# Multiplying the expert weights into identity blocks on GpSimd, ahead of ScalarE's diagonals

## The reference, cut to what matters

```python
def one_chunk(args):                       # 128 tokens
    hc, ec, gc = args                      # tokens, expert indices (128, 8, 16), softmax weights
    pre = jnp.einsum('cd,chkd->chk', hc, u[ec]).astype(jnp.float32)
    coef = (gc * jax.nn.gelu(pre, approximate=False)).astype(h.dtype)
    return jnp.einsum('chk,chkd->cd', coef, v[ec])
```

## Time and profile before

| what | value |
|---|---|
| three runs | 2333.66 us median (2331.21 to 2335.54) |
| profiled execution | 2334.32 us, span of its instructions 2332.6 us |
| PE, PEld, DVE busy | 84%, 58%, 60% of the span |
| ACT, POOL busy | 46%, 25% |
| gathers | from 354.4 us on; the last matmul of a row ends at about 1957 us |
| mean granted TensorE clock | 0.905 |

### The profile page before, as it was taken

How to read it: one execution, slowest core, us unless ns; L and a number is a source line. 1 busy time by engine, 2 the same in 40 slices (tenths; PEclk the granted TensorE clock), 3 DMA queues, 4 the chain that set the end, 5 groups by cost and what they waited for, 6 DMA issues and landing times.

```text
span 2332.6 us, 41079 instructions
## 1 busy us (share of the span) xinstructions
PE 1959.3 (84%) x16124; PEld 1344.2 (58%) x16124; DVE 1395.7 (60%) x3264; ACT 1074.3 (46%) x2533; POOL 582.4 (25%) x541
## 2 busy tenths in 40 slices
PE   5888897988888779877855988889888885999999
PEld 4767785655545546545522623356665553667887
DVE  6654678686776676656577576666555533123554
ACT  3334545455555652224344758634454213343443
POOL 0000003332223343334344234433333330000000
PEclk8999998998888889998966996689999997999999
DMA  9932449998889999999999999999999994313555
GB/s 343 340 123 73 162 136 386 390 385 340 322 326 409 402 418 418 417 419 418 417 418 414 410 396 402 382 418 417 418 417 418 418 418 173 137 46 127 183 180 169
DMA packets 140497, 758.52 MB, mean 325 GB/s; under 512 B 16224, under 2 KB 22496, under 8 KB 74384
## 3 DMA queue, kind: packets, MB, share of 16 engines
q0 software_dynamic: 74784, 543.30, 57.1%
q1 hardware_dynamic: 60864, 208.23, 24.0%
q10 hardware_dynamic: 4656, 4.36, 0.6%
HBM read 751.60 MB, written 4.23 MB: 324 GB/s over the span
## 4 chain that ended last, share of the span: by engine, by line
PE 44%; DMA 30%; ACT 10%; DVE 10%; issue 4%; POOL 2%; ACTq 0%; SPq 0%; DVEq 0%
DMA arena<-experts,eidx 27%; PE psum L1324 7%; PE psum L842 4%; DVE arena L2475 4%; PE psum L843 4%; PE psum L844 4%; PE psum L1172 4%; DMA ring<-w_stream 2%; POOL arena L2452 2%; PE psum L1448 2%; PE psum L1621 2%; PE psum L1498 2%; DVE ring_low L2495 2%; ACT arena L2096 1%; PE psum L1197 1%
## 5 line engine op out<-in xcount | busy, mean ns | idle before, releaser
L2475 DVE CUSTOM_DVE_ANT_0 arena<-arena 128x1024 f32<-128x1024 f32 (+3 forms) x592 | 691.6, 1182 | 398.5 <-DMA arena<-experts,eidx 372.1
L2452 POOL DMA_INDIRECT arena<-experts,eidx x512 | 573.6, 1120 | 1203.8 <-PE psum L1324 925.6
L1324 PE MATMUL psum<-arena,sq 32*32 32x512 f32 x8192 | 372.2, 710 | 278.4 <-ACT sq L2104 265.6
L2090 ACT ACTIVATE arena<-arena 128x2 f32<-128x2 f32 x256 | 51.8, 202 | 585.5 <-DVE arena L2475 582.7
L1324 PEld LDWEIGHTS psum<-arena,sq 32*32 32x32 f32 x8192 | 84.4, 110 | 402.7 <-ACT sq L2104 351.0
L1172 PE MATMUL psum<-arena,ring 128*128 128x256 f32 x976 | 235.5, 396 | 4.1 <-ACT arena L1945 4.1
L1172 PEld LDWEIGHTS psum<-arena,ring 128*128 128x128 f32 x976 | 187.3, 197 | 77.1 <-issue 47.3
L1643 PE MATMUL psum<-arena,ring 128*128 128x256 f32 x704 | 162.6, 386 | 0.7 <-DVE arena L2472 0.7
L842 PE MATMUL psum<-hn_high,w_high 128*128 128x256 f32 (+1 forms) x416 | 127.8, 307 | 39.6 <-DVE ring_low L2495 21.7
L1643 PEld LDWEIGHTS psum<-arena,ring 128*128 128x128 f32 x704 | 131.2, 191 | 48.6 <-issue 31.0
L2104 ACT ACTIVATE sq<-sq,arena 128x32 f32<-128x32 f32 x512 | 136.6, 314 | 23.8
(11 more groups left out here) (377 smaller groups left out, 3380.6 us busy)
## 6 DMA issues: line engine op xcount, KB each, us to landing
ring<-w_stream SPq DMA_DIRECT2D x340, 512.0 KB
arena<-w_ada SPq DMA_DIRECT2D x48, 512.0 KB, 7.2
arena<-experts,eidx POOLq DMA_INDIRECT x512
arena<-cum_rows POOLq DMA_DIRECT2D x1, 2112.0 KB, 10.2
x<-xT SPq DMA_DIRECT2D x2, 1024.0 KB, 8.5
arena<-rel_rows ACTq DMA_DIRECT2D x4, 512.0 KB, 12.7
arena<-rel_rows POOLq DMA_DIRECT2D x1, 1024.0 KB, 10.7
k_early<-arena POOLq DMA_DIRECT2D x2, 512.0 KB, 6.3
```

The source lines that it names most:

```text
L1324: last = mm(bank(4 + 2 * odd + a)[QUART * b:QUART * b + QUART, :], diag[k, s, :], rows[k, s, D + a * 512:D + (a + 1) * 512], start=c == 0, ...
L2090: steps(op(pre[:, s:s + 2], pre[:, s:s + 2], ACT.Gelu))
L2452: nc.gpsimd.indirect_dma_start(rows[:, s, :], None, experts, bass.IndirectOffsetOnAxis(ap=eidx[:, n // P % 2, n % P:n % P + 1], axis=0)).t ...
L2475: return V.tensor_tensor_reduce(out=out, in0=a, in1=b, scale=1.0, scalar=0.0 if op1 == ALU.add else -TAKEN, op0=op0, op1=op1, accum_out=accum)
```

## The change

GpSimd gets an instruction for each pair of rows: it multiplies `ident_quart` by the two columns of `wgt`, into a new buffer `weighted_ident` of 8 blocks of 32 columns (the last 256 columns of `sq`). ScalarE makes the diagonals from these blocks, scaled by the Gelu in `pre`; its two multiplications into `coef` go. The waits for `weighed` and `pair_ready` move from ACT to POOL. POOL's order is: gathers 0 to 7, the blocks for rows 0 to 7, then gather(n), and after each even one weigh(n). A block is free again when ACT has made the diagonals of the two rows that used it 8 rows before.

```diff
+        weighted_ident = sq_flat[:, SQ_FREE + T:SQ_FREE + T + SLOT * QUART].rearrange("p (a b) -> p a b", b=QUART)
...
                 steps(op(pre[:, s:s + 2], pre[:, s:s + 2], ACT.Gelu))
-                if n % PK == 0:
-                    act.wait_ge(weighed.sem, weighed.ready(n // PK))
-                steps.wait()
-                for c in range(2):
-                    k = (n + c) % P
-                    steps(op(coef[:, s + c:s + c + 1], pre[:, s + c:s + c + 1], ACT.Copy,
-                             scale=wgt[:, n // P % 2, k:k + 1]))
                 if n >= SLOT:
                     act.wait_ge(rows_used.sem, rows_used.free(n + 1, SLOT))
+                act.wait_ge(ident_weighed.sem, ident_weighed.ready(n // 2))
                 steps.wait()
-                if n == 0:
-                    act.wait_ge(pair_ready.sem, pair_ready.ready(0))
                 for c in range(2):
-                    op(diag[:, s + c, :], ident_quart, ACT.Copy, scale=coef[:, s + c:s + c + 1]).then_inc(diag_done.sem, 1)
+                    op(diag[:, s + c, :], weighted_ident[:, s + c, :], ACT.Copy, scale=pre[:, s + c:s + c + 1])\
+                        .then_inc(diag_done.sem, 1)
...
+            def weigh(n):
+                s, k = n % SLOT, n % P
+                if n == 0:
+                    pool.wait_ge(pair_ready.sem, pair_ready.ready(0))
+                if n % PK == 0:
+                    pool.wait_ge(weighed.sem, weighed.ready(n // PK))
+                if n >= SLOT:
+                    pool.wait_ge(diag_done.sem, diag_done.free(n + 1, SLOT))
+                nc.gpsimd.tensor_tensor(weighted_ident[:, s:s + 2, :], ident_quart.unsqueeze(1).to_broadcast([P, 2, QUART]),
+                                        wgt[:, n // P % 2, k:k + 2].unsqueeze(2).to_broadcast([P, 2, QUART]), ALU.mult)\
+                    .then_inc(ident_weighed.sem, 1)
...
-            for n in range(HEADS * PK):
+            for n in range(SLOT):
                 gather(n)
+            for n in range(0, SLOT, 2):
+                weigh(n)
+            for n in range(SLOT, HEADS * PK):
+                gather(n)
+                if n % 2 == 0:
+                    weigh(n)
```

More of the change, by code:

```diff
@@ L675, in program @@
         diag_done = signal("act", "diag_done")
+        ident_weighed = signal("pool", "ident_weighed")
         rows_used = signal("pe", "rows_used")
@@ L2090, in diagonals @@
                 steps(op(pre[:, s:s + 2], pre[:, s:s + 2], ACT.Gelu))
-                if n % PK == 0:
-                    act.wait_ge(weighed.sem, weighed.ready(n // PK))
+                if n >= SLOT:
+                    act.wait_ge(rows_used.sem, rows_used.free(n + 1, SLOT))
+                act.wait_ge(ident_weighed.sem, ident_weighed.ready(n // 2))
                 steps.wait()
                 for c in range(2):
-                    k = (n + c) % P
-                    steps(op(coef[:, s + c:s + c + 1], pre[:, s + c:s + c + 1], ACT.Copy,
-                             scale=wgt[:, n // P % 2, k:k + 1]))
-                if n >= SLOT:
-                    act.wait_ge(rows_used.sem, rows_used.free(n + 1, SLOT))
-                steps.wait()
-                if n == 0:
-                    act.wait_ge(pair_ready.sem, pair_ready.ready(0))
-                for c in range(2):
-                    op(diag[:, s + c, :], ident_quart, ACT.Copy, scale=coef[:, s + c:s + c + 1]).then_inc(diag_done.sem, 1)
+                    op(diag[:, s + c, :], weighted_ident[:, s + c, :], ACT.Copy, scale=pre[:, s + c:s + c + 1])\
+                        .then_inc(diag_done.sem, 1)
             def sum_out(j):
@@ L2454, in gather @@
                     bass.IndirectOffsetOnAxis(ap=eidx[:, n // P % 2, n % P:n % P + 1], axis=0)).then_inc(rows_ready[s], 16)
-            for n in range(HEADS * PK):
-                gather(n)
+            def weigh(n):
[4 more added lines that the diff above has]
+                    pool.wait_ge(weighed.sem, weighed.ready(n // PK))
+                if n >= SLOT:
+                    pool.wait_ge(diag_done.sem, diag_done.free(n + 1, SLOT))
[3 more added lines that the diff above has]
+            for n in range(SLOT):
+                gather(n)
+            for n in range(0, SLOT, 2):
[4 more added lines that the diff above has]
+                    weigh(n)
             pool.wait_ge(cum_ready.sem, cum_ready.ready(1))
```

## The result

The changed kernel is faster: 2315.75 us median of 7 runs (2307.74 to 2324.1) against 2331.59 us of the kernel before in 7 runs (2331.21 to 2338.36), ratio 0.993, 95% interval 0.991 to 0.9951. A second set, 10 runs beside 33 of the kernel before, gave 2315.86 against 2333.66 us, ratio 0.992 (0.9891 to 0.9949). Ratios leave out single runs over 1.5% above the fastest of their kernel, medians are of all runs. The profiled execution took 2315.75 us, its span 2314.0.

What follows compares the result with a forecast made beforehand. Full DMA queues were taken to bound the kernel, gains coming only where transfers rest. The terms 6.6 - 1.6 + 2.0 + 0.55 + 0.5 - 0.9 = 7.15 us off 2334.32 gave 2327 us, ratio 0.997, range 2317 to 2337.

Steps and rivals of the forecast that it cites:

- What bounds the kernel: Row loop: full DMA queues set the time; only stretches where DMA rests can gain, 40.6 us of rest in all.
- The part that goes: Between Gelu and diagonal on ScalarE: without the copies, 0.55 us less for each pair on the chain.
- 520 to 700 us: Early resting stretch: 12 chain passes at 0.55 us, 6.6 us, less 1.6 us taken back by other work.
- 1380 to 1500 us: Late stretch: 8 chain passes, 4.4 us, DMA resting only 4.3 us; 2.0 us taken, bounds 0 and 4.3.
- rival 3: 520 to 700 and 1420 to 1500 us: fewer stalls keep TensorE's clock up; 17 us in all, 2317 us; chance 0.12.
- The halves that were assumed: Resting stretches: only 20 chain passes counted at 0.55 us, 6.6 us cut by a quarter, 4.4 us to 2.0.
- The part that is added: GpSimd's 256 multiplications: 0.6 us each with gap, delay hidden by queue or row ahead; held dots cost 0.9 us.
- The port: Shared SBUF ports: a two-input VectorE instruction and a GpSimd one wait for each other; at most 12 us over 40 pairs.
- rivals 4 and 5: VectorE held by the multiplication in resting stretches, 2344 us, chance 0.09; POOL becoming the bound everywhere, 2462 us, chance 0.05.
- The tail and the rest: Last pair, copy between last Gelu and last matmuls: 0.55 us; remaining small DMA rests: 0.5 us, bounds 0 and 7.0.
- Rival 1: The forecast itself: 4.7 to 11 us faster, 2323 to 2329 us, from chain passes in 520 to 700 us; chance 0.45.
- rival 2: 520 to 700 us: TensorE's own list takes back three quarters of 6.6 us; 3.8 us or less, 2330 to 2334; chance 0.29.

Runs made afterwards that it cites:

- copies_rest: Changed kernel with the two old copies back between Gelu and diagonal for 64 pairs, rows 64 to 111 and 304 to 383: 2330.93 us, 1.0001.
- copies_full: Changed kernel with the two old copies back for the other 192 pairs, out for rows 64 to 111 and 304 to 383: 2319.69 us, 0.9941.
- copies_early: Changed kernel with the two old copies back between Gelu and diagonal for rows 64 to 111 alone, 24 pairs: 2321.13 us, ratio 0.9935.
- pool_only: Kernel before with GpSimd's 256 multiplications added and read by nobody, ScalarE as before: 2335.06 us, ratio 1.0008.
- act_only: Changed kernel without GpSimd's multiplication; diagonals are identity blocks scaled by the Gelu, experts' weights left out: 2316.4 us, ratio 0.9927.
- copies_behind: Changed kernel with two 128x1 copies of constants put on ScalarE behind the two diagonals: 2320.81 us, ratio 0.9939.
- weigh_twice: Changed kernel with GpSimd's multiplication done twice for each pair: 2319.96 us, ratio 0.9938.
- weigh_four: Changed kernel with one multiplication for four rows, behind the fourth gather, 128 instructions in place of 256: 2318.58 us, ratio 0.9933.
- copies_late: Changed kernel with the two old copies back between Gelu and diagonal for rows 304 to 383 alone, 40 pairs: 2323.37 us, ratio 0.9946.
- copies_rest_double: Changed kernel with four copies instead of two between Gelu and diagonal for 64 pairs, rows 64 to 111 and 304 to 383: 2345.94 us, 1.0047.

## Why the prediction was right and wrong

**What bounds the kernel: right.** Only pairs in stretches where transfers rest count. copies_rest and copies_full show it from both sides, and 820 to 1260 us keeps 416 to 419 GB/s in every variant.

**The part that goes: right in kind, 0.49 us a pair instead of 0.55.** The wait ahead of the diagonal did not go with the copies.

**520 to 700 us: right.** The forecast had 6.6 - 1.6 = 5.0 us; copies_early gave back 5.3 us, not told from none by its interval. That the size fits is partly luck: the chain passes through L2096 11 times in this stretch, not 12 (6.05 us, not 6.6), and the quarter taken off was a guess. Between gathers 64 and 128 five profiles with the long way in all or the early rows took 214.3, 209.3, 211.1, 206.3 and 215.7 us (before twice, pool_only, copies_rest, copies_early), eight with the short way 203.8, 209.6, 210.2, 203.1, 211.4, 201.5, 201.5 and 206.1 (the changed kernel twice, act_only, copies_behind, copies_full, weigh_twice, weigh_four, copies_late). The means are 211.3 and 205.9, 5.4 us apart, with a scatter about as large.

**1380 to 1500 us: the step that failed.** The forecast took 2.0 us of 4.4, bounded by 4.3 us of rest, and at most 3.0 us for 1260 to 1380 us. The runs show 6 to 7.5 us there. copies_late gave back 7.5 us by the medians. Rows 304 to 383 took 229.2, 227.7, 231.5, 227.7 and 229.0 us in the profiles with the long way there (before twice, pool_only, copies_rest, copies_late) and 221.5, 225.4, 221.1, 227.9, 222.0, 222.0, 220.5 and 221.1 in those with the short (the changed kernel twice, act_only, copies_behind, copies_full, weigh_twice, weigh_four, copies_early). The means are 229.0 and 222.7, 6.3 us apart. That makes some 4 to 5.5 of the 9 to 11 us by which the sum was short; the rest of them is in no one place, with 2 to 3 us behind the last gather.

Three things in that step were wrong. The rest was worked out from the DMA share, 0.96 and 0.99 in the earlier trace rows, and where the share is 0.99, the rate is 400 and not 418 GB/s: the share hides a part of what is lost. By the rate, 381 of 418 GB/s, the rest in 1420 to 1500 us is 80 x (1 - 381 / 418) = 7.1 us, and with 1260 to 1380 us, 120 x (1 - 400 / 418) = 5.2 us, 12.3 us, where I allowed 7.3 in all and took 2.5. Over rows 304 to 383 the rates of the fences above give 10.4 us of rest before and 2.6 and 7.0 in the two profiles of the changed kernel. Second, I halved the term because most of the rest came after the last of the eight passes. But a pair early in the stretch that is 0.49 us quicker can make all that follows it earlier; this is argued, no run separates it. Third, the term held nothing for TensorE's clock, which was left to rival 3. In the late rows PE's idle time did not shrink; its busy time did, by 8.3 us, at a higher granted clock. Whether the clock carried the gain or followed it stays open.

**The halves that were assumed.** The way was worth about half its length in time (copies_rest_double), for 64 pairs. The forecast counted 20 pairs at 0.55 and took a quarter to a half off. The 20 passes (19 by the trace) of the one printed chain through L2096 were too few: taking 0.5 us off 64 pairs or adding it moved the time by 15 us, as 30 such pairs would.

**The part that is added: right.** The multiplication costs 513 ns mean instead of 300, 0.16 us of gap behind it, and at times a whole dot; nothing of it is seen in the time (pool_only 1.0008, act_only no better than the whole change, twice as much no different by its interval). The gather behind it is late; that the queue covers it is argued from this.

**The port.** The page "SBUF — State Buffer" of the Trainium skill, section "Who interferes with whom", was weighed as a rival. Both directions are now in the traces. In the timeline above, a dot issued at 612.16 under a multiplication that runs to 612.39 takes 1.31 us instead of 1.22. The trace has 33 dots that start under a multiplication, with 0.22 us of it left in the median; they take 1.30 us in the median, and the more was left, the longer they take. The group of dots in the changed kernel and that of multiplications, ns:

```profile
L2489 DVE CUSTOM_DVE_ANT_0 arena<-arena x528: 541/1225/1412, 362.8 to 1937.1; 128x1024 f32<-128x1024 f32 x171, 128x384 f32<-128x384 f32 x3, 128x512 f32<-128x512 f32 x2
```

```profile
L2460 POOL TENSOR_TENSOR sq<-sq,arena x256: 283/311/1346, 367.4 to 1920.4; 128x64 f32<-128x64 f32 x128
```

The multiplication is at 0.3 us in the median and up to 1.35 when a dot holds it; the longest dot is 1412 ns where it was 1280. The median dot, 1225, has not moved, but the mean of the 560 of 128x1024 went from 1221 to 1232 ns, 6.6 us in all. The rule agrees with the trace, but for some 0.1 us: a held dot grows by that much less than what was left of the multiplication. Its price in the kernel's time is not told from none: rivals 4 and 5 fell.

**The tail and the rest.** 0.55 us for the last pair and 0.5 for other rests are below what these runs can tell. 15.1 of 17.8 us are found by putting the copies back in 64 pairs; the other 2.7 us are within the intervals.

**The rivals.** Rival 1, the forecast with its range of 2323 to 2329, and rival 2 fell. Rival 3, more by the clock, has the size right (2317) and agrees with PE's busy time in the late rows, but it is not shown: the clock does rise with the shorter way, and raising it by added matmuls cost as much PE time as it gave. How much of the 6 to 7.5 us of the late rows comes through it stays open, since a stretch with the same matmuls and another clock can't be made without touching PE's work or its waits.

## What to carry to other kernels

Where a transfer queue is full, work taken off another engine is worth little or nothing; 94 us of it moved the time by 4, not told from none. Find the stretches where the queue rests and measure the rest by the rate, bytes moved against the full rate, not by the busy share. In such stretches of this kernel a shortened pass was worth about half its length on average over 64 pairs, and not only the 19 passes that the printed chain goes through counted. Look also at whether a stretch got shorter by less waiting or by shorter busy time of the same work.

Before explaining a stretch by one profile, take a second one of the same kernel: 5 us here, a quarter of the gain, was one profile's own.

## What the runs showed of the hardware

GpSimd's multiplication of 128 x 64 took 283 ns at least, and one of 128 x 128 (weigh_four) 391:

```profile
L2460 POOL TENSOR_TENSOR sq<-sq,arena x128: 391/408/1481, 366.1 to 1913.9; 128x128 f32<-128x128 f32 x128
```

That is 108 ns for 64 more columns, 1.7 ns each, and by a line through both about 175 ns that do not depend on the size.

An indirect gather is held by a VectorE instruction with two inputs as well: 1.77 us at 612.55 in the changed kernel, against 0.94 for most in the earlier trace rows's stretch, with a dot running from 612.16 to 613.47. That is 0.83 us more, the dot's remainder of 0.92 us less 0.09.

TensorE's granted clock over rows 336 to 383 went from 0.66 to 0.87 by matmuls that compute nothing, with no change in the time of the stretch: the other matmuls took 25 us less and the added ones 25.9.
